# A Fourier mixer of half the width, with its loads, its modulation rows and its held groups rearranged

## The reference

```python
# block 1 (mixer is fourier_mix, no context)
sh1, sc1, g1, sh2, sc2, g2 = split(silu(c) @ w_mod + b_mod, 6)        # w_mod is 2048 x 12288
h   = rms_norm(x, norm_g[0]) * (1 + sc1) + sh1
y   = fftn(h.reshape(L, 8, 256), axes=(tokens, 256)).real @ fnet_w_out  # per group of 256 features
x   = x + g1 * rms_norm(y, norm_g[1])
x   = x + g2 * rms_norm(relu(m(x) @ w_mlp_in)**2 @ w_mlp_out, norm_g[3]) # m: rms_norm, (1 + sc2), + sh2
# block 2: gated linear attention, forgetting attention (FoX, causal) and memory attention
o   = concat(gla, fox, mem); h = x + (o * gate) @ w_out
out = h + relu(rms_norm(h) @ w_up)**2 @ w_down                         # hidden width 8192
```

## Time and profile before

| | |
|---|---|
| median of 3 runs | 2138.3 us |
| the profiled execution's own time | 2136.71 us |
| its span (first to last instruction) | 2135.0 us |
| TensorE busy | 2092.3 us, 98% |
| VectorE, ScalarE busy | 1356.6 us, 994.9 us |
| data moved | 492.26 MB, 231 GB/s over the span, 387 to 397 GB/s in the first 200 us |
| granted TensorE clock, mean | 0.997 |

### The profile page before, as it was taken

The page is one execution under the profiler, slowest core; times in us unless marked ns, Lnnn a source line. Parts: engine busy times, 40 slices in busy tenths (PEclk is TensorE's granted clock), DMA queues, the critical chain, the costliest instruction groups (busy, mean ns, idle before and its releaser), DMA issues.

```text
span 2135.0 us, 29831 instructions
## 1 busy us (share of the span) xinstructions
PE 2092.3 (98%) x11099; PEld 1762.9 (83%) x11099; DVE 1356.6 (64%) x1350; ACT 994.9 (47%) x1282; POOL 59.2 (3%) x95
## 2 busy tenths in 40 slices
PE   5999999999999999999999999999999999999999
PEld 3767878888888888887988888888888888888887
DVE  3878988887655655656767476555645655554563
ACT  4344364444543444444554567554434434343442
POOL 0010000110000000001100000000000000000000
PEclk9999999999999999999999999999999999999999
DMA  9999988887667667666665555566566656656654
GB/s 387 379 393 397 371 320 329 305 303 259 223 213 213 214 213 221 207 223 199 207 179 158 149 159 186 190 185 187 191 193 188 191 192 189 191 191 194 189 189 156
DMA packets 222842, 492.26 MB, mean 231 GB/s; under 512 B 15148, under 2 KB 15528, under 8 KB 221976
## 3 DMA queue, kind: packets, MB, share of 16 engines
q1 hardware_dynamic: 211956, 450.98, 64.9%
q0 software_dynamic: 10112, 38.79, 5.4%
...
## 4 chain that ended last, share of the span: by engine, by line
PE 87%; DVE 5%; DMA 2%; ACT 2%; issue 2%; SPq 1%; DVEq 0%; ACTq 0%
PE ps L559 43%; PE ps L521 22%; PE ps L526 11%; DVE acc L1662 3%; DMA raw<-in_w_mod_dram 2%; PE ps L543 1%; PE ps L544 1%; PE ps L545 1%; PE ps L608 1%; DMA raw<-in_w_mem_kv_dram 1%; PE ps L821 1%; PE ps L820 1%; PE ps L819 1%; PE ps L967 1%; SPq L310 1%
## 5 line engine op out<-in xcount | busy, mean ns | idle before, releaser
L1637 DVE TENSOR_TENSOR wl<-raw,wh 128x1024 fp32r<-128x1024 f32 x684 | 810.4, 1222 | 283.6 <-ACT wh L1140 281.5
L1140 ACT ACTIVATE wh<-raw 128x1024 fp32r<-128x1024 f32 x684 | 697.4, 1054 | 526.2 <-DMA raw<-in_w_down_dram 159.9
L521 PE MATMUL ps<-xt,wh 128*128 128x512 f32 x2048 | 643.7, 396 | 1.4 <-DVE xt L1897 1.4
L559 PE MATMUL ps<-wh,u 128*128 128x512 f32 x2176 | 585.1, 389 | 1.0 <-DVE u L2224 0.6
L559 PEld LDWEIGHTS ps<-wh,u 128*128 128x128 f32 x2176 | 407.3, 188 | 85.8 <-DVE u L2224 1.0
L526 PEld LDWEIGHTS ps<-xt,wl 128*128 128x128 f32 x2048 | 384.7, 188 | 90.9
L526 PE MATMUL ps<-xt,wl 128*128 128x256 f32 x2048 | 402.3, 278 | 0.0
L559 PE MATMUL ps<-wl,u 128*128 128x512 f32 x1088 | 335.2, 389 | 0.0
L521 PEld LDWEIGHTS ps<-xt,wh 128*128 128x128 f32 x2048 | 312.2, 189 | 2.8 <-issue 2.4
L559 PE MATMUL ps<-wh,xt 128*128 128x512 f32 x960 | 269.0, 394 | 3.9 <-DVE wl L1637 2.6
L559 PEld LDWEIGHTS ps<-wl,u 128*128 128x128 f32 x1088 | 204.2, 188 | 42.5
...
## 6 DMA issues: line engine op xcount, KB each, us to landing
raw<-in_w_mlp_in_dram SPq DMA_DIRECT2D x128, 512.0 KB, 4.0
raw<-in_w_mlp_out_dram SPq DMA_DIRECT2D x128, 512.0 KB, 4.3
raw<-in_w_up_dram SPq DMA_DIRECT2D x128, 512.0 KB, 3.8
raw<-in_w_down_dram SPq DMA_DIRECT2D x128, 512.0 KB, 3.6
raw<-in_w_mod_dram SPq DMA_DIRECT2D x126, 512.0 KB, 10.5
raw<-in_w_in_dram SPq DMA_DIRECT2D x96, 512.0 KB, 3.8
slot<-in_w_mod_dram POOLq DMA_DIRECT2D x32, 512.0 KB, 5.2
raw<-in_w_out_dram SPq DMA_DIRECT2D x32, 512.0 KB, 3.6
```

What stands on the lines that cost most here:

```text
L521: mm(ps[:, 4 * par + j, :], wh[:, at, t, j * P:(j + 1) * P], flat(xt[:, kt, :, :]), start=kt == 0, stop=kt == KT - 1, skip_group_check=True)
L559: last = mm(o, act[:, kt, z, half * P:(half + 1) * P], w, start=kt == 0 and n == 0, stop=kt == KT - 1 and n == 2, skip_group_check=True)
L1140: A(flat(wh[:, i, :, :]), tile_at(landed[0]), ACT.Copy).then_inc(sem("w_hi"), 1)
L1637: V.tensor_tensor(flat(low_at(s)), tile_at(s), flat(wh[:, i, :, :]).bitcast(F32), ALU.subtract).then_inc(sem("w_lo"), 1)
```

## The change

Seven things are changed at once.

1. Token transform: only frequencies 0 to 129 of each half are computed (`NF` is 129, one column is padding), 260 columns per matmul in place of 512.
2. Feature transform: groups are taken in pairs. The cosine part has 2 x 129 = 258 columns, the sine part 2 x 127 = 254, and there are 4 x 24 matmuls in place of 8 x 24. Both parts are summed apart in one PSUM bank; ScalarE copies the sine part out (`fm_parts`), VectorE forms difference and sum for the two halves of the frequencies (`fm_sum`), and ScalarE and VectorE split the result as before.
3. `AHEAD` is 8: eight fn chunks are loaded among the last eight tiles of `g1`. TensorE now takes tiles 0 to 27 of `g1` (before: 0 to 3 and 8 to 27), the last four of them behind fn3.
4. `TAIL` begins with the first four `sh2` tiles, before the MLP's chunks. VectorE leaves the last four `sc2` tiles until the residual is done, and makes the diagonals before it takes up the sum of `sc2`.
5. `sh2`: TensorE takes 4 tiles rather than 8. Its sum over partitions is one matmul per 512 columns (`row_sum`) into two partitions; ScalarE copies that row out (`summed_row`), and GpSimd sends it to DRAM and back, turned to one value per partition and column (`turned_row`, elements of 4 bytes). The same way is used for the bias of the held groups.
6. All four held groups are made from unshifted activations; 32 tiles are reloaded. The `g2` tiles that VectorE took in the first eight groups are moved to the down projections behind them.
7. FoX skips the keys that the mask hides: 8 of its 16 half blocks of queries and keys become narrower in the scores and the product, and 4 of 16 transposes go.

The diff, cut to what the text speaks of:

```diff
+NF = S // 2 + 1
+PAIRS = 4
...
 SC1_QUADS = tuple(n for n in range(32) if n // QUAD not in (3, 7))
-G1_QUADS = tuple(n for n in range(32) if n // QUAD not in (1, 7))
+G1_QUADS = tuple(n for n in range(32) if n // QUAD != 7)
...
-AGAIN_EACH = 4
+SH2_QUADS = tuple(n for n in range(32) if n // QUAD == 0)
+AGAIN = [(pair, kt) for pair in range(2) for kt in range(KT)]
...
-AHEAD = 4
+AHEAD = 8
...
-        TAIL = ([("chunk", j) for j in range(4)] + [("tile", n) for n in range(4)]
+        TAIL = ([("tile", n) for n in range(4)] + [("chunk", j) for j in range(4)]
                 + [item for j in range(4, HEAD) for item in (("chunk", j), ("tile", j))]
                 + [("tile", n) for n in range(HEAD, MODN)])
...
+            def turned_row(k, dst, src, scratch, half):
+                pool.wait_ge(sem("turn_rows"), k + 1)
+                if k:
+                    pool.wait_ge(sem("turn_in"), 16 * k)
+                pool.dma_start(scratch[half].rearrange("(j n) -> j n", n=GC),
+                               src[0:2 * QP:QP, half * MODC:half * MODC + GC]).then_inc(sem("turn_out"), 16)
+                pool.wait_ge(sem("turn_out"), 16 * (k + 1))
+                pool.dma_start(dst[:, half * CH:(half + 1) * CH], scratch[half].rearrange("(c p) -> p c", p=P),
+                               allow_slow_non_contiguous=True).then_inc(sem("turn_in"), 16)
...
+            shift_row(0)
+            pool.wait_ge(*mod_used(mod_c(C_SH2, MODN - 1)))
+            for r in range(4):
+                again_tile(r)
+            shift_row(1)
+            for r in range(4, 20):
+                again_tile(r)
+            side_tile(0, 0)
+            for r in range(20, 23):
+                again_tile(r)
...
                 for dt in range(2):
-                    o = ps[:, tok_bank(g) + dt, :]
...
                         for z, t in ((0, dfth), (0, dftl), (1, dfth)):
-                            last = mm(o, xn[:, z, half, d0:d0 + P], t[:, half, :], start=half == 0 and z == 0 and t is dfth,
+                            last = mm(o, xn[:, z, half, d0:d0 + P], freqs(t[:, half, :])[:, :, 0:NF + 1], start=half == 0 and z == 0 and t is dfth,
...
-                if g >= 2:
-                    pe.wait_ge(sem("fm_lo"), g - 1)
+            def dft_features(q):
...
+                pe.wait_ge(sem("p_lo"), q + 1)
+                if q >= 2:
+                    pe.wait_ge(sem("fm_sum"), q - 1)
...
-                    o = ps[:, g % 2, dq * S:(dq + 1) * S]
+                    o = ps[:, pair_bank(q) + dq, :]
                     for kt in range(2):
                         for part in range(2):
                             lhs = slice(part * S + dq * P, part * S + (dq + 1) * P)
-                            mv_ = slice(part * S, (part + 1) * S)
...
+                            cols = slice(2 * NF, 2 * S) if part else slice(0, 2 * NF)
+                            start = kt == 0 and part == 0
+                            mm(o[:, cols], dfth[:, kt, lhs], pdft[:, q % 2, kt, 0, cols], start=start, stop=False, skip_group_check=True)
+                            mm(o[:, cols], dftl[:, kt, lhs], pdft[:, q % 2, kt, 0, cols], start=False, stop=False, skip_group_check=True)
+                            last = mm(o[:, cols], dfth[:, kt, lhs], pdft[:, q % 2, kt, 1, cols], start=False,
...
             mod_rows("g1", C_G1, 0, 2)
-            for g in range(8):
-                dft_features(g)
-                if g in G1_ROWS_AT:
-                    n = G1_ROWS_AT[g]
+            mod_rows("g1", C_G1, 4, 2)
+            for q in range(PAIRS):
+                dft_features(q)
+                for n in G1_ROWS_AT[q]:
                     if n == KT:
                         pe.wait_ge(sem("tok_out"), 8)
...
-                    if (g, i) == (0, 4):
+                    if (g, i) == (0, 3):
+                        mod_rows("g1", C_G1, 24, 4)
...
             pe.wait_ge(sem("evacuated"), G_ML1 - 1)
             mod_rows("sh2", C_SH2, 0, 2)
             pe.wait_ge(sem("evacuated"), G_ML1)
+            pe.wait_ge(sem("sq"), 12)
...
                 if (g, i) in ((0, 0), (0, 1)):
                     transposes(1, h, (2 + i,), drained="x1t_out")
-                if (g, i) == (1, 4):
+                if (g, i) == (1, 5):
                     pe.wait_ge(*mod_used(mod_c(C_SH2, KT - 1)))
...
-                    mod_sum(2, 0, (0,))
-                if (g, i) == (2, 1):
-                    pe.wait_ge(sem("evacuated"), G_ML1 + 2)
-                    mod_rows("sh2", C_SH2, KT, 4)
+                    row_sum(acc2, 0, 0)
                 if (g, i) == (3, 5):
                     pe.wait_ge(*mod_used(mod_c(C_SH2, MODN - 1)))
                     pe.wait_ge(sem("evacuated"), G_ML1 + 3)
-                    mod_sum(2, 0, (1,))
+                    row_sum(acc2, 1, 0)
...
+            def row_sum(t, half, bank):
+                for j in range(2):
+                    last = mm(ps[j * QP:(j + 1) * QP, bank, :], ones[:, 0:QP], t[:, half * MODC + j * GC:half * MODC + (j + 1) * GC],
+                              start=True, stop=True, skip_group_check=True, tile_position=(0, j * QP))
+                last.then_inc(sem("turn_mm"), 1)
...
+                        if g in (2, 4) and i == 0:
+                            pe.wait_ge(sem("turn_rows"), g // 2)
...
+            def keys_of(name, tb):
+                return (tb + 1) * P if name == "fox" else S
...
+                        for sb_ in range(keys_of(name, tb) // P):
...
+            def fm_parts(q):
+                act.wait_ge(sem("dft_d"), q + 1)
+                A(fm(q)[:, :, :, 0:NF:NF - 1], even_sums(q, slice(0, NF, NF - 1)), ACT.Copy)
+                A(fmq(q), ps[:, pair_bank(q):pair_bank(q) + 2, 2 * NF:2 * S].rearrange("p d (g n) -> p g d n", g=2),
+                  ACT.Copy).then_inc(sem("fm_part"), 1)
+            def fm_hi(q):
+                act.wait_ge(sem("fm_sum"), q + 1)
+                A(turned_rows(q, 0), fm(q), ACT.Copy).then_inc(sem("fm_hi"), 1)
...
+            h_squares(0)
+            root(4)
             hi_static(CH * G_ML1)
             hi_static(CH * G_ML1 + 1)
-            h_squares(0)
-            root(4)
             act.wait_ge(sem("a2_ready"), 1)
...
+            def fm_sum(q):
+                dve.wait_ge(sem("fm_part"), q + 1)
+                t = fm(q)
+                V.tensor_tensor(t[:, :, :, 1:NF - 1], even_sums(q, slice(1, NF - 1)), fmq(q), ALU.subtract)
+                V.tensor_tensor(t[:, :, :, S - 1:NF - 1:-1], even_sums(q, slice(1, NF - 1)), fmq(q),
+                                ALU.add).then_inc(sem("fm_sum"), 1)
...
+            def fm_lo(q):
+                dve.wait_ge(sem("fm_hi"), q + 1)
+                V.tensor_tensor(turned_rows(q, 1), fm(q), turned_rows(q, 0).bitcast(F32), ALU.subtract).then_inc(sem("fm_lo"), 1)
+            for q in range(PAIRS):
+                fm_sum(q)
+                if q + 2 < PAIRS:
+                    p_lo_rest(q + 2)
+                    p_lo_first(q + 2)
+                if q == 2:
                     fold("g1", C_G1, 0, 0, 2)
...
-            for n in range(MODN - AHEAD, MODN):
+            for n in range(MODN - AHEAD, MODN - 4):
                 gemv("sc2", C_FN, n, 1)
...
             for piece in range(4):
                 residual(piece)
+            for n in range(MODN - 4, MODN):
+                gemv("sc2", C_FN, n, 1)
+            mean(2, 4, "hsq", 4)
+            diagonals()
             mod_vector(3, vtmp[:, :], 7)
             link(V.tensor_scalar(vtmp[:, :], vtmp[:, :], 1.0, None, ALU.add))
             V.tensor_tensor(a2[:, :], v("ng2", KT), vtmp[:, :], ALU.mult).then_inc(sem("a2_ready"), 1)
-            mean(2, 4, "hsq", 4)
-            diagonals()
```

More of the change, by code:

```diff
@@ new lines, in shift_row, with bias_row @@
+            def shift_row(half):
+                turned_row(half, s2, acc2, s2_dram, half)
+            def bias_row(pair):
+                turned_row(2 + pair, hb, acc[1], hb_dram, pair)
+            shift_row(0)
[8 more added lines that the diff above has]
+                again_tile(r)
@@ L470, in _ @@
-            with pool.Fori((GQ + len(AGAIN) // AGAIN_EACH) // 2, QT * GQ) as n2:
+            with pool.Fori(2 * GQ, QT * GQ) as n2:
                 for half in range(2):
@@ L1148, in hi_run @@
                 for j in range(CH):
-                    if between and j < 5:
+                    if between:
                         between(j)
@@ L1247, in _ @@
             p_hi(0)
-            for g in range(8):
-                if g < 7:
-                    p_hi(g + 1)
-                if g == 0:
+            p_hi(1)
+            for q in range(PAIRS):
+                if q == 0:
                     tok_out(7)
-                if g == 6:
+                fm_parts(q)
+                if q + 2 < PAIRS:
+                    p_hi(q + 2)
+                if q == PAIRS - 1:
                     hi_static(CH * G_FN)
-                fm_hi(g)
-                if g == 6:
+                fm_hi(q)
+                if q == PAIRS - 1:
```

(10 more changed lines are left out.)

329 lines of the change are left out of this document (174 added, 155 removed).

## The result

The changed kernel takes 2150.9 us as the median of four runs (2149.5 to 2155.4), the kernel before 2138.45 beside it: a ratio of 1.0062, 95% interval 1.0049 to 1.0075. It is **12.4 us slower**. The forecast was 2139.0, a change of +0.6 us, with a range of 2130 to 2151; the time lies at the range's upper edge. Of the three outcomes "slower" had the largest chance (0.40, against 0.36 for no change), but a good half of that (0.23) stood for rival A, which is not what happened. The profiled execution has a span of 2149.3 us, 14.3 more than before.

What follows compares the result with a forecast made beforehand. TensorE was taken to bound the kernel from 284 us on, the order of loads ahead of that. Terms -5.0 + 10.2 - 7.1 + 2.5 = +0.6 us gave 2139.0 us, range 2130 to 2151.

Steps and rivals of the forecast that it cites:

- rival A: Feature transform: matmuls under 256 columns leave the fast rate, 16 us more for 48 sine matmuls; 2149, chance 0.23.
- Step 1: Transforms: fewer matmul columns and earlier fn loads bring S at about 163.6, 9.2 us earlier.
- S: Time of the output projection's first matmul: 172.81 us before, forecast 163.6.
- Step 2: Output projection: added mod_rows pass 1.9 us and slot waits 2.3, nothing else; T at 260.0, -5.0 us.
- T: End of the output projection's last chunk, fn31: 265.02 us before, forecast 260.0.
- Step 3: Turn to the MLP: TensorE idle behind residual and four gemv, plus clock loss; first MLP matmul at T + 28.3, +10.2 us.
- M: Time of the first MLP matmul: T + 18.1 before, forecast T + 28.3.
- Step 4: Behind 284 us: fewer matmuls in the sh2 pass, sums over partitions and FoX; -7.1 us.
- Step 5: Held groups: shift row through DRAM comes late, a wait at group 4's fifth chunk; +2.5 us.
- B: Output projection, turn and held groups: no slot stall, clock back at once, shift row in time; -6.0, 2132, chance 0.22.
- C: Shift row's way through DRAM takes longer, wait reaches 7 us; 2143.5, chance 0.15 together with D.
- D: Halved feature transform worth nothing as loads end last; S only 5.2 us earlier; 2143, chance 0.15 together with C.

Runs made afterwards that it cites:

- e9: e5 with 12 float32 matmuls without use added behind each pair of the feature transform; 2136.8 us.
- e1: Changed kernel with tiles 24 to 27 of g1 on VectorE and TensorE's pass behind fn3 gone; 2143.8 us.
- e2: Changed kernel with the gate's second half moved four steps later; 2146.1 us.
- e3: Changed kernel with the last four sc2 tiles taken by VectorE ahead of the residual again; 2139.3 us.
- e10: Changed kernel with AHEAD 4 and tiles 24 to 27 of g1 taken by TensorE ahead of the fn chunks; 2146.9 us.
- e5: Changed kernel with the edits of e1, e2 and e3 together; 2132.7 us.
- e6: Changed kernel with AHEAD 4, tiles 24 to 27 on TensorE ahead of the fn chunks, and the edits of e2 and e3; 2130.7 us.

## Why the prediction was wrong

**Step 1, S: right**, by 0.3 us. Its path is right too: the first fn chunk's load ends last, and ScalarE takes it at 161.40 (162 forecast). That the last pair ended at 158.9 and not at 161 changed nothing, since it was not what S waited for. e9 shows why the 11.5 us of matmuls could not all come out.

**Step 2, T: the step that failed.** It put T at 260.0, with -7.3 and -1 us as bounds; it came out at +7.2. From S to T it had 96.4 us, and 108.4 were measured. The stop of SyncE was seen, and the two waits that it makes were put at the right chunks, fn6 and fn8, with 1.6 and 2.2 us; they were 2.82 and 2.09. Its end was put at about 176 and came at 180.74, since fn2 and fn3 had waited 3.28 us ahead of the pass, and the load behind it took 5.7 us where 4.0 were taken. So the stop itself was mis-sized by 1.1 us only. What was left out makes the rest: 3.28 us for the waits at fn2 and fn3, whose cause stays open; 2.66 us for the gate's wait; and 3.4 us of low clock, for which nothing was charged. The remaining 1.3 us are unassigned. e1 puts 7.1 us on the stop and the pass, with the clock behind them.

"Nothing else" was wrong: the order of VectorE's work had put the second gate half one chunk behind the first, which the list of the change does not name, and the gains of both halves come through one slot. A round trip (free, issue, land) is 216.13 - 209.1 = 7.0 us, and a chunk 2.7: e2 puts 4.8 us on it. It could be read from the order alone: before, the halves stood three chunks apart (8.3 us, and the second waited for nothing), after, one. VectorE's timeline before:

```profile
191.77 1.23 DVE L1828 TENSOR_TENSOR acc<-ps,slot 128x1024 f32<-128x1024 f32 x1 [0.72 <-PE ps L744]
...
200.03 1.22 DVE L1828 TENSOR_TENSOR acc<-ps,slot 128x1024 f32<-128x1024 f32 x1
```

**Step 3, the turn: the mechanism right, the size off.** The idleness was 13.6 us (13.3 forecast) and e3 gives 11.6 us by moving the four tiles. The clock's term was mis-sized: 1.8 us were charged (the row that it came from gives 1.7), one low stretch like that in the earlier trace rows, where 3.3 (`mod_sum`) + 1.7 (`mod_rows`) + 0.5 (`keep_busy`) = 5.5 were lost. The earlier trace rows show `mod_rows` alone slow because `mod_sum` had run ahead of the wait there; here both stood behind it. M came at T + 32.3, the upper bound named (+14) to 0.2 us.

**Step 4: right** in the profile of the changed kernel, -7.1, in its parts 4.9 and 2.2. Of the other profiles only that of e10 repeats it; in the rest the same stretch is 1.5 to 5.9 us shorter than before, with VectorE's waits described at e5. **Step 5: wrong, to no harm**: no wait at the fifth chunk of group 4 where 2.5 us were charged. The way through DRAM took 395.01 to 404.36 = 9.3 us for the second half of the row, where 11 were taken; ScalarE waited 3.4 us for it and TensorE not at all.

The sum: 12.3 (step 2) + 3.9 (step 3) - 2.5 (step 5) = 13.7 above the forecast of the profiled execution's time, 2137.3; it was 2150.95.

**The rivals.** A's time (2149) was near the measured one by luck, for A is false: 254 columns run like 258, in the changed kernel's feature transform 282 and 284 ns by form, each 0.12 us from start to start:

```profile
157.97 0.28 PE L789 MATMUL ps<-pdft,dfth 128*128 128x254 f32 x1
158.09 0.28 PE L787 MATMUL ps<-pdft,dfth 128*128 128x258 f32 x1
158.21 0.28 PE L788 MATMUL ps<-pdft,dftl 128*128 128x258 f32 x1
```

B is false, though in e5 and e6 something near its time was reached by undoing three orders. C is false: the turned loads landed 3.2 to 4.4 us after their issue, not 6.8 or more. D is false as it was put, since the halving did move S; that the loads cover a part of it is true (e9).
